# Two fused transformer blocks in fp32 on one core: the second modulation group goes through the hi/lo split, and the squares of x and context are summed one step further on VectorE

## The reference, cut to what matters

```python
mod_l = (jax.nn.silu(c) @ w_ada[l] + b_ada[l])[:, None, :]
mod_c = (jax.nn.silu(c_ctx) @ w_ada[l] + b_ada[l])[None, None, :]
sh_a, sc_a, gt_a, sh_f, sc_f, gt_f = jnp.split(mod_l, 6, axis=-1)
...
h_l = modulate(rms_norm(x, g_mix_norm[l]), sh_a, sc_a)
h_c = modulate(rms_norm(xc, g_mix_norm[l]), csh_a, csc_a)
qa_l, kva_l, kr_l, cb_l, cc_l, ch_l = split_projection(h_l @ w_in[l])
```

## Time and profile before

| | |
|---|---|
| Time, median of 3 runs | 2312.01 us (2311.33 to 2312.95) |
| Time of the profiled execution | 2311.34 us |
| Its span, first to last instruction | 2309.6 us |
| TensorE busy | 2261.1 us, 98% |
| VectorE busy | 1577.1 us, 68% |
| ScalarE busy | 1078.1 us, 47% |
| Mean rate of the transfers | 204 GB/s |

### The profile page before, as it was taken

How to read it: one execution, slowest core, us unless ns; L and a number is a source line. 1 busy time by engine, 2 the same in 40 slices (tenths; PEclk the granted TensorE clock), 3 DMA queues, 4 the chain that set the end, 5 groups by cost and what they waited for, 6 DMA issues and landing times.

```text
span 2309.6 us, 36780 instructions
## 1 busy us (share of the span) xinstructions
PE 2261.1 (98%) x16168; PEld 2079.6 (90%) x16168; DVE 1577.1 (68%) x1838; ACT 1078.1 (47%) x1067; POOL 41.9 (2%) x80
## 2 busy tenths in 40 slices
PE   8899999999999999999999999999999999999998
PEld 3679878999999988888888989999999999999998
DVE  3977997989786456665667778775576545445674
ACT  4655344434444345543554444445354436654352
POOL 0000000000000000000000000000000000000000
PEclk9999999999999999999999999999999999999999
DMA  9775875795775555555555444334445554335443
GB/s 380 288 273 222 312 285 220 299 367 210 273 269 218 186 184 195 186 182 192 192 182 203 162 177 155 144 129 162 167 165 182 183 182 146 120 137 183 168 161 128
DMA packets 64944, 471.69 MB, mean 204 GB/s; under 512 B 7216, under 2 KB 7216, under 8 KB 8336
## 3 DMA queue, kind: packets, MB, share of 16 engines
q1 hardware_dynamic: 55152, 399.21, 47.2%
q0 software_dynamic: 9488, 68.03, 7.8%
q10 hardware_dynamic: 144, 2.10, 0.2%
HBM read 467.21 MB, written 2.10 MB: 203 GB/s over the span
## 4 chain that ended last, share of the span: by engine, by line
PE 80%; DVE 13%; ACT 3%; issue 3%; DMA 1%; DVEq 0%; ACTq 0%; SPq 0%
PE acc L1996 61%; PE aux L1996 19%; DVE lo L1018 4%; ACT hi L425 2%; DVE ada_acc L1038 2%; DMA ada_raw<-ada_stream 1%; DMA raw<-stream 1%; DVE x L1849 0%; DVE x L1846 0%; DVE rstd L1156 0%; ACT probs L819 0%; DVE act_both L1856 0%; DVE columns L1779 0%; ACT y L508 0%; DVE probs L1775 0%
## 5 line engine op out<-in xcount | busy, mean ns | idle before, releaser
L1018 DVE TENSOR_TENSOR lo<-raw,hi 128x2048 fp32r<-128x2048 f32 x366 | 835.9, 2289 | 519.8 <-ACT hi L425 519.2
L425 ACT ACTIVATE hi<-raw 128x2048 fp32r<-128x2048 f32 x366 | 698.1, 1911 | 771.2 <-PE acc L1996 648.7
L1996 PE MATMUL acc<-act_both,hi 128*128 128x256 f32 (+1 forms) x7552 | 1013.0, 291 | 16.6 <-ACT hi L425 4.9
L1996 PEld LDWEIGHTS acc<-act_both,hi 128*128 128x128 f32 x7552 | 957.1, 192 | 47.0 <-issue 17.5
L1996 PE MATMUL acc<-act_both,lo 128*128 128x256 f32 x3984 | 520.8, 283 | 0.4 <-DVE lo L1018 0.2
L1996 PEld LDWEIGHTS acc<-act_both,lo 128*128 128x128 f32 x3984 | 498.4, 192 | 3.1 <-DVE lo L1018 1.1
L1038 DVE SCALAR_TENSOR_TENSOR ada_acc<-ada_raw,silu_c,ada_acc 128x512 f32<-128x512 f32 x224 | 152.9, 745 | 5.4 <-DMA ada_raw<-ada_stream 5.2
L1996 PE MATMUL aux<-act_both,hi 128*128 128x512 f32 (+1 forms) x512 | 118.8, 377 | 0.0
L1996 PEld LDWEIGHTS aux<-act_both,hi 128*128 128x128 f32 x512 | 91.9, 189 | 15.9
L1996 PE MATMUL acc<-u_both,hi 128*128 128x512 f32 (+1 forms) x536 | 99.5, 339 | 0.0
L1996 PEld LDWEIGHTS acc<-u_both,hi 128*128 128x128 f32 x536 | 82.5, 190 | 9.7
(11 more groups left out here) (338 smaller groups left out, 1795.7 us busy)
## 6 DMA issues: line engine op xcount, KB each, us to landing
raw<-stream SPq DMA_DIRECT2D x374, 1024.0 KB, 4.8
ada_raw<-ada_stream POOLq DMA_DIRECT2D x64, 1024.0 KB, 6.1
x<-x_t SPq DMA_DIRECT2D x1, 2048.0 KB, 15.7
ctx<-ctx_t SPq DMA_DIRECT2D x1, 2048.0 KB, 13.5
x<-x_t ACTq DMA_DIRECT2D x1, 2048.0 KB, 8.8
out<-x SPq DMA_DIRECT2D x3, 512.0 KB, 7.5
p_raw<-p_t POOLq DMA_DIRECT2D x1, 512.0 KB, 4.3
out<-x SPq DMA_DIRECT2D x2, 256.0 KB, 2.1
```

Of the source, the lines that this page charges most:

```text
L425: nc.scalar.activation(HI[c % NH][:, :], RAW[c % NR][:, :], ACT.Copy).then_inc(hi_done, 1)
L1018: V.tensor_tensor(LO[c % NR][:, :], RAW[c % NR][:, :], HI[c % NH][:, :].bitcast(F32), ALU.subtract)\
L1996: return TE.matmul(out, lhs, rhs, start=start, stop=stop, skip_group_check=True)
```

## The change

`WHOLE` becomes 1, so chunks 4 to 7 (group 4, the first scales) take the way of `hi` and `lo`: ScalarE copies them, VectorE subtracts, TensorE multiplies with four weight columns (`silu_c_split`), hi and then lo. In ScalarE's loop the root of x and the squares of the context move from p = 4 to p = 6, which is behind the copies of chunks 6 and 7. And `tree` adds a second level, 128 x 1024 floats, so that TensorE's sum over the partitions has four matmuls in place of eight, for x and for the context.

```diff
-WHOLE = 2
+WHOLE = 1
...
-                if p == 4:
+                if p == 6:
                     in_root("nx", 0)
                     act.wait_ge(sem("ctx_loaded"), 16)
                     squares("nc", CTX, SQC)
...
                 dve.wait_ge(*since(name + "_sq", 2))
-                V.tensor_tensor(src[:, 0:8, :], src[:, 0:8, :], src[:, 8:16, :], ALU.add)\
+                link(V.tensor_tensor(src[:, 0:8, :], src[:, 0:8, :], src[:, 8:16, :], ALU.add))
+                V.tensor_tensor(src[:, 0:4, :], src[:, 0:4, :], src[:, 4:8, :], ALU.add)\
                     .then_inc(step(name + "_ss")[0], 1)
...
                 pe.wait_ge(*since(name + "_ss", 1))
-                for k in range(8):
-                    ins = mm(AUX[:, bank, 0:T], ONES[:, :], src[:, k, :], k == 0, k == 7)
+                for k in range(4):
+                    ins = mm(AUX[:, bank, 0:T], ONES[:, :], src[:, k, :], k == 0, k == 3)
                 ins.then_inc(step(name + "_tot")[0], 1)
```

## The result

| | before | changed |
|---|---|---|
| Median, 10 runs each | 2312.98 us (2311.28 to 2313.38) | 2318.49 us (2315.26 to 2320.71) |
| Ratio | | 1.0024, 95% interval 1.0016 to 1.0033 |
| Profiled execution, its span | 2311.34, 2309.6 us | 2315.26, 2313.5 us |
| Mean granted clock in it | 0.997 | 0.993 |

The changed kernel is 5.5 us slower, and the interval lies wholly above 1. The profiled execution is the fastest of its ten runs, so the traces, 3.9 us apart, show less than the medians do.

What follows compares the result with a forecast made beforehand. In the first 55 us TensorE and transfers are both full, so chunk landings decide. Profiled 2311.34 + 5.8 us at `enter_x` = 2317.1, plus 0.7 to the median: 2317.7 us forecast, range 2316.2 to 2318.9, with rivals 2314.3 to 2319.7.

Steps and rivals of the forecast that it cites:

- the cap: First `enter_x`, behind chunk 11's landing and copy: can't begin before 47.8 against 49.05, so at most 1.2 us won.
- The chain: Start: chunk 7's landing, copy, subtraction, variance, root, squares, context's tree, three subtractions, scales; `enter_x` at 54.15, 5.1 us late.
- The clock's term: TensorE behind a 7.1 us pause before the context's total: low clock loses 1.6 to 2.6 us, `enter_x` at 54.4 to 55.3.
- the 2.6 of the start: Program start, behind 6.72 us of nothing: 8 records took 6.16 us against 3.46 later, read as 2.6 us lost.
- That upper end: Clock loss of 2.6 us in the context's total and chunk 8: chunk 8 ends at 53.3, `enter_x` at 55.3.
- the +5.8: Summed delay at first `enter_x`, 54.85 against 49.05, with ends +5.1 and +6.3; without the clock rule +5.1.
- the rival of transfers that a later start finds landed: Between 54 and 165 us, ScalarE's chunk waits take back 3.3 us, delay shrinks to 2.5: 2314.5; chance 0.22.
- the 1.2 us from which the rival would decide: Delay taken back behind `enter_x` from which the rest is within 0.2% (4.6 us), not told from no change.

Runs made afterwards that it cites:

- e1: Changed kernel with the context's squares and their tree moved ahead of chunk 6; ratio 1.0012 to the kernel before.
- e5: Changed kernel without the subtractions and low products of chunks 4, 5 and 6; ratio 1.0019 to the kernel before.
- e6: Kernel before, nothing split, with the variance of x held back on VectorE behind chunk 7's landing and two added additions; ratio 1.0028 to the kernel before.
- e4: Changed kernel with eleven unread matmuls filling TensorE's pause between chunk 7 and the context's total; ratio 1.0023 to the kernel before.
- c1: The changed kernel measured once more, unaltered, on a second chip; ratio 1.0022 to the kernel before.
- e3: Kernel before with only the split of chunks 4 to 7 and the moved root and squares, tree at one level; ratio 1.0030 to the kernel before.

## Why the prediction was right

**What bounds the start.** That both TensorE and the transfers were full, and that TensorE's unbroken chain hid it, was the right reading: the chain after the change runs through the landing of chunk 7 (18.22 to 34.57), and the tree alone, which spares TensorE 3.7 us, gets 1.14 us at `enter_x` where 1.2 was the cap.

**The chain.** Forecast and measured: copy of chunk 7 at 34.8 and 34.59; variance 39.0 and 38.75; tree of the context 43.5 and 43.25; VectorE free for chunk 8 at 47.05 and 46.72. All are 0.2 to 0.3 early, since the first landing is (the vectors' 3.69 instead of 3.86 on ScalarE). `enter_x` was put at 54.15 by VectorE and 54.4 to 55.3 by TensorE, and came at 54.17, by TensorE. That order and not load makes it is shown by e1, e5 and e6 together.

**The clock's term was too large at `enter_x`.** I had the pause at 7.1 us; it was 5.18, because TensorE was slow already between 26 and 36 us, which I had not seen coming, and so finished chunk 7 at 41.7 instead of 39.9. The loss behind the pause was 1.5 us, as behind the pause of 3.9 us in the earlier trace rows and not the 2.6 of the start. That upper end was weak from the outset: the first records of the program do take twice as long as later ones, but the profile's clock reads 1.00 from 6 to 16 us, so those rows don't show a low clock. At `enter_x` the +5.8 was +5.1, and without the low clock it is +4.8 (e4).

**What happens behind it.** The forecast was that all later rows keep the delay. In the first profile they keep +5.12 us through the second `enter_x` (86.78 to 91.90) and +5.13 at the third (121.17 to 126.30). At the fourth, 149.41 to 153.71, it is 4.3, and before `act_both` of line 691, 533.81 to 537.42, it is 3.6. The first drop looks like the rival of transfers that a later start finds landed, in small. ScalarE's waits for a chunk there, before and after:

```profile
140.72 1.92 ACT L425 ACTIVATE hi<-raw 128x2048 fp32r<-128x2048 f32 x1 [0.44 <-DMA raw<-stream]
144.72 1.92 ACT L425 ACTIVATE hi<-raw 128x2048 fp32r<-128x2048 f32 x1 [1.61 <-DMA raw<-stream]
```

```profile
145.65 1.92 ACT L425 ACTIVATE hi<-raw 128x2048 fp32r<-128x2048 f32 x1 [0.25 <-DMA raw<-stream]
148.64 1.92 ACT L425 ACTIVATE hi<-raw 128x2048 fp32r<-128x2048 f32 x1 [0.60 <-DMA raw<-stream]
```

The wait of 1.61 us is one of 0.60. But the other traces don't bear this reading out. The tree alone, which starts 1.1 us early, waits 1.17 us there and is 1.6 early at the fourth `enter_x` (147.83); the split alone, 6.3 late, is 6.6 late there (156.06). And at `act_both` e5 stands at +3.6, but e4, e6 and c1 at +6.6, +7.6 and +12.8. What becomes of the delay behind 130 us differs from one execution to the next by more than the 1.2 us from which the rival would decide, and in no trace is more than 1.5 us of it gone by `act_both`, where the rival had 3.3 by 165 us. So the rival as it was priced has fallen, and a small part of it is neither shown nor excluded. The second drop in the first profile falls near 435 us, where TensorE waits 0.42 us for a reciprocal before (at 437.28) and not at all after (440.98).

**The sum.** 2317.7 forecast, 2318.49 measured. The mechanism was right, but that the two numbers lie so near is in part luck. The forecast was 2317.1 for the profiled execution and 0.7 us from there to the median. The profiled execution came at 2315.26, 1.9 us lower: 0.7 us of clock too much at `enter_x`, and 1.2 us that this trace takes back behind it (+5.1 there, +3.9 at its end). The median then lies 3.2 us above it (1.6 in the kernel before), and for these 2.5 us more the prediction had no term. The second ten runs, on another chip, put the change at +4.6 us.

That the changed kernel's runs spread more (5.5 us against 2.1) fits its lower mean clock; it was not tested apart. e4, which spares one low stretch, spreads only 2.6 us, but e1 and e3 on the same chip spread 2.6 and 2.5 without the filler, so this shows nothing.

**The whole change.** It gives TensorE 10.1 us of work back in a stretch where TensorE is held up by landings, and pays with VectorE work whose place in the order puts the norm of x behind the last landing of the group. By halves: the tree alone -1.3 us, within its uncertainty, the split alone +7.4, where both together have +4.6 to +5.5. None of the variants beats the kernel before by more than can be told; the tree alone is the best of them.

## What to carry to other kernels

An engine that is busy without a gap need not be the bound: look whether the transfers are full in the same windows, and ask of each saving what lands next. When work is added to an in-order engine, price the instructions that now stand behind it by when its input lands, not by how long it takes; and when a chain seems to be set by the order, move an independent piece into the wait, and see whether the engine's own load takes over as the limit.

## What the runs showed of the hardware

TensorE's clock fell not only in one long pause. In the changed kernel, behind waits of 2.71 and 2.98 us with 1.09 us of work between them (21.6 to 28.4 us), the granted clock was 0.54 from 26 to 28 us and 0.50 from there to 36 us, while TensorE was busy 3.60 of the 4 us from 28 to 32 and all of the 4 us from 32 to 36. The total of x took 3.2 us to the next group for it. In the tree alone, where TensorE doesn't wait there, the clock is 1.00 from 24 to 40 us. In e1, with the same work between waits of 1.58 and 2.97 us, it is 1.00 from 24 to 28, 0.53 from 28 to 32 and 0.62 from 32 to 36 us: it fell later and for less time. Even waits of 1.16 and 1.71 us around the same work were followed by 0.50 from 30 to 32 us (e3). Eleven matmuls that nobody reads, put into the later pause, kept the clock up behind it (1.54 us for the same total).
